# When the low parts of two weight chunks are made, in a three-block model kernel with a ring of weight slots

## The chip, the cores and the metric

The kernel runs on one core of one Trainium2 chip. The metric is the device time of one execution in microseconds, as the median of several runs; smaller is better. A profile of one execution stands beside it.

## The reference

A batch of one with 256 tokens (and 256 context tokens), width 1024. The first part is two layers, each with modulation, a mixer (attention), a layer norm, a gated feed-forward with a width-3 convolution, and a second layer norm. The second part puts 16 meta tokens ahead (272 tokens), and runs one layer of state-space mixing and a mixture of experts, with RMS norms. Everything is float32.

```python
def conv_ffn(h, w_gate, w_up, conv_w, conv_b, w_down):
    g = h @ w_gate
    ...
    return (jax.nn.silu(g) * (h @ w_up)) @ w_down

def first_block(...):
    for i in range(DEPTH):                       # 2 layers
        mods = modulation(c, w_mod[i], b_mod[i]) # one more set for the context
        h = x * (1.0 + sc1) + sh1
        o = even_mixer(...) if i % 2 == 0 else odd_mixer(...)
        x = layer_norm(ALPHA * x + gt1 * o, ln1_g[i], ln1_b[i])
        h = x * (1.0 + sc2) + sh2
        x = layer_norm(ALPHA * x + gt2 * conv_ffn(h, ...), ln2_g[i], ln2_b[i])
    return x

def second_block(x, meta_tokens, ...):
    h = concatenate([meta, x])
    u = rmsnorm(h, norm_mix)
    proj = u @ w_in
    h = h + concatenate([ssd_branch(proj...), short_conv_branch(proj...)]) @ w_out
    h = h + hier_moe(rmsnorm(h, norm_ffn), ...)
    return rmsnorm(h, norm_final)[:, N_META:]
```

## The kernel before

Activations lie feature-major: eight pieces of 128 features by 512, 256 or 272 tokens. The weights come as one list of chunks (`chunk_plan`), nearly all 128 x 2048 floats (1 MB), in the order of their use. SyncE walks the list and starts one DMA for each chunk into a ring of three slots, so chunk n takes the slot of chunk n - 3. It waits until `slot_free` says that this chunk is done with.

A float32 product is made from three products of rounded operands (type float32r): high by high, high part of the weight by low part of the input, low part of the weight by high part of the input (`mm3`). So each chunk is split: ScalarE copies it from the ring into WH (`act_high`, L461), VectorE subtracts to make WL (`dve_low`, L471); there are three places for split chunks. Once the low part is made, the chunk's ring slot is free. Chunks of the kinds `mod`, `qb` and `kvb` are not split (`whole`): TensorE reads them in the ring, and their slot is free when their product is done.

```python
        def slot_free(m):
            key = plan[m][0]
            if key[0] == "mod":
                return at("used", m)
            return at(*whole_free[key]) if whole[m] else at("low", m)
```

TensorE, ScalarE, VectorE and SyncE each run a program written out in order; they meet only at counted marks (`up`, `at`). The `ahead` argument of `act_high(e, n, ahead)` and `dve_low(e, n, ahead)` says how many chunks of the list, from n, are split at that point of the engine's program, unless they are already.

The places that matter, in order of time:
- Output projection and n00. `pe_out` multiplies `about` 0 to 3, VectorE adds each piece into X (`dve_out`, L800), and statistics of the layer norm follow. `pe_norm` spreads the mean and the deviation over the partitions (L602). Around them it multiplies modulation chunks of the second layer (`pe_mod`, L517): for n00 mod 1,0 and mod 1,1 ahead, mod 1,2 behind. VectorE and ScalarE make the eight normed pieces and split them (`dve_norm` L701, L719, L724; `act_norm` L669, L673).
- First feed-forward. The chunk list here reads about 3; gu 0,0; gu 0,1; mod 1,0; mod 1,1; mod 1,2; gu 0,2; mod 1,3; gu 0,3; and so on (gu l,f holds 128 columns of gate and of up of layer l). `four_tiles` multiplies gu 0,0 and gu 0,1 together, piece by piece as the norm delivers them; then each further chunk makes two tiles. The same list ends in 8 `down` chunks for each half.
- n01 and the second mixer's inputs: down 0,1,7; din 4; din 5; mod 1,21; mod 1,22; mod 1,23; din 6. `pe_norm` multiplies mod 1,21 and mod 1,22 ahead and mod 1,23 behind; `four_tiles` takes din 4 and din 5.
- n10 and the second feed-forward, dout 3; gu 1,0; gu 1,1; gu 1,2, with no modulation chunks between.
- n11 and block two: `pe_win` sums the squares of eight pieces (`pe_stat`, L597), spreads the root (L602), multiplies win 0 and win 1 in `four_tiles` and win 2 to 11 tile by tile; a small product by token (`pe_by_token`, L1726) lies between. The squares are VectorE's (L1824), the sum with the bias is ScalarE's (L2771).

Today, low parts are made ahead of a norm as follows. In `dve_out` of a norm's input, the last but one chunk makes low parts up to the second split chunk after it, and the last chunk does likewise. So the low parts of both chunks of `four_tiles` exist before the norm.

Of the kernel before, what the change touches and what calls it, by code (L numbers as in the profile page):

```python
# [17 lines left out]
NT = 272  # L18
# [324 lines left out]
def build(nc, wts, xin, meta, vecs, conds, csts, out):  # L343
# [5 lines left out]
    with ExitStack() as ctx:  # L349
# [129 lines left out]

        def mm3(e, o, w, cols, x, k, nk):  # L480
            e.matmul(o, w[0][:, cols], x[0], start=k == 0, stop=False)  # L481
            e.matmul(o, w[0][:, cols], x[1], start=False, stop=False)  # L482
            return e.matmul(o, w[1][:, cols], x[0], start=False, stop=k == nk - 1)  # L483
# [10 lines left out]
        def four_tiles(e, cs, o, x, names, arrive):  # L494
            ws = [weights(e, c) for c in cs]
            for k in range(8):
                e.wait_ge(*at(*arrive, k))
                for c, w, oc, name in zip(cs, ws, o, names):
                    for m in range(2):
                        t = mm3(e, oc[m], w, slice(256 * k + 128 * m, 256 * k + 128 * m + 128), at_k(x, k), k, 8)  # L500
                        if k == 7:
                            t.then_inc(*(up("used", c) if m else up("tile", *name)))
# [127 lines left out]
        def pe_norm(e, N, between=()):  # L630
            for c in between[:-1]:
                pe_mod(e, 1, c)
            b = bank(e, "mean", N.tag)
            e.wait_ge(*at("variance.mean", N.tag))
            pe_spread(e, b, N.MU, N.q).then_inc(*up("mean", N.tag))
            banks.give(b, "scaled.centered", N.tag, 7)
            b = bank(e, "unit_dev", N.tag)
            e.wait_ge(*at("variance.inverse", N.tag))
            pe_spread(e, b, N.RS, N.q).then_inc(*up("mean.unit_dev", N.tag))
            banks.give(b, "scaled", N.tag, 7)  # L640
            for c in between[-1:]:
                pe_mod(e, 1, c)
# [143 lines left out]
        def dve_out(e, key, n, mt_per, l, gt, tag, nxt):  # L786
            for i in range(8 // mt_per):
                c = index[key + (i,)]
                dve_low(e, c, next_pair(c) if tag in NORMS and i >= 8 // mt_per - 2 else 2)
# [29 lines left out]
        def pe_ffn(e, F_):  # L819
            l, n = F_.l, F_.n  # L820
            H = parts(8, n)
            for half in range(2):
                if half == 0:
                    bs = [(bank(e, "gate", l, f), bank(e, "up", l, f)) for f in range(2)]
                    four_tiles(e, [index["gu", l, f] for f in range(2)], [[ps[:, b, 0:n] for b in bf] for bf in bs], H,
                               [("gu", l, f) for f in range(2)], ("norm_low", F_.arrive))
# [17 lines left out]

        def act_ffn(e, F_, put_off):
            l, n = F_.l, F_.n
            H2 = ffn_parts(n)
            for half in range(2):
                for i in range(HALF):
# [3 lines left out]
                    act_high(e, c)  # L853
# [19 lines left out]
        def dve_ffn(e, F_, gt_from, fold_next=None):  # L873
# [3 lines left out]
            for half in range(2):  # L877
                for i in range(HALF):
# [5 lines left out]
                    dve_low(e, c)  # L884
# [806 lines left out]
        def pe_stat(e, tag, j, sq):  # L1691
            e.wait_ge(*at("stat_square" if tag == "mix" else "stat_square_act", tag, j))
# [17 lines left out]
        def dve_stat_norm(e, tag, gname, dst):  # L1710
# [6 lines left out]
            for j in range(8):  # L1717
                e.scalar_tensor_tensor(out=dst[:, j, :], in0=R[:, j, :], scalar=V(gname, j),
                                       in1=B("stat_spread", tag)[:, 0:NT], op0=ALU.mult,
                                       op1=ALU.mult).then_inc(*up("normed", tag, j))  # L1720

        def pe_by_token(e, tag, w, n, row, arrive):
# [5 lines left out]
            banks.give(b, "token.row", tag)  # L1728
            b = bank(e, "tokens.turned", tag)
# [25 lines left out]
        def pe_win(e):  # L1755
            bank(e, "stat", "mix")
            for j in range(8):
                pe_stat(e, "mix", j, ZS)
            bs = [[bank(e, "win", 2 * i + m) for m in range(2)] for i in range(2)]
            four_tiles(e, [index["win", i] for i in range(2)], [[ps[:, b, 0:NT] for b in bi] for bi in bs], YP,  # L1760
                       [("win", 0), ("win", 2)], ("u_low",))
            for i in range(12):
# [8 lines left out]
                if i == 1:  # L1771
                    pe_by_token(e, "dt", "wdt", 16, sc_root, "mix")

        def act_win(e):
            e.wait_ge(*META)
            e.wait_ge(*at("residual", "n11", 7))
            e.activation(R[:, :, 0:16], MT.rearrange("p (a b) -> p a b", a=8), ACT.Copy).then_inc(*up("joined"))
            act_stat_root(e, "mix")
# [3 lines left out]
            for i in range(12):  # L1782
# [4 lines left out]
                if i == 1:  # L1787
                    act_time(e)
# [29 lines left out]
        def dve_win(e):  # L1818
# [3 lines left out]
            for j in range(8):  # L1822
                e.wait_ge(*at("residual", "n11", j))
                e.tensor_tensor(ZS[:, j, 16:NT], R[:, j, 16:NT], R[:, j, 16:NT],  # L1824
                                ALU.mult).then_inc(*up("stat_square", "mix", j))
            dve_stat_norm(e, "mix", "nmix", UB)
            for j in range(8):
                e.wait_ge(*at("u_high", j))
                e.tensor_tensor(YP[1][:, j, :], UB[:, j, :], YP[0][:, j, :].bitcast(F32),
                                ALU.subtract).then_inc(*up("u_low", j))  # L1830
            for i in range(12):
# [4 lines left out]
                if i == 1:  # L1836
                    dve_time(e)
# [10 lines left out]
        def dve_time(e):  # L1848
            dve_token_row(e, "dt", 16, sc_root)
# [514 lines left out]
        def pe_gather(e):  # L2364
            pe_by_token(e, "ffn", "rw", 20, RSTD, "ffn")
            for c in range(3):
# [363 lines left out]
        def tensor_program(e):  # L2730
# [9 lines left out]
            pe_norm(e, N10)  # L2740
            pe_ffn(e, F1)
            pe_norm(e, N11)
# [11 lines left out]
        def scalar_program(e):  # L2754
# [14 lines left out]
            for j in range(8):  # L2769
                e.wait_ge(*at("scaled", "n11", j))  # L2770
                e.activation(R[:, j, 16:NT], N11.T8[:, j, :], ACT.Identity, bias=V("ln2b1", j),  # L2771
                             scale=1.0).then_inc(*up("residual", "n11", j))
# [139 lines left out]
```

## Time and profile before

| | us |
|---|---|
| median of 3 runs | 1879.32 (1878.71 to 1881.64) |
| the profiled execution | 1878.08 |
| its span in the profile | 1876.3 |
| TensorE busy | 1750.7 |
| VectorE busy | 1075.4 |
| ScalarE busy | 827.8 |
| mean granted TensorE clock | 0.951 of full |

Starts in the timelines are microseconds from the start of the span. A matmul's shown duration includes its passage through the array; products in a row overlap, so the distance between starts is what one costs. The granted clock of 1.00 is 2.4 GHz, 0.50 is 1.2 GHz; a value between means that the stretch saw both.

### The profile page before, as it was taken

The page shows a single profiled execution, that of the slowest core. Times are in us where ns is not written, and L with a number is a line of the kernel's source. Part 1 is how long each engine was busy: PE and PEld are TensorE (multiplying, and loading weights), DVE is VectorE, ACT ScalarE, POOL GpSimd, SP SyncE. Part 2 cuts the span into 40 slices and gives each one's busy share as a digit, 9 for nine tenths or more (in the row PEclk, how much of TensorE's full clock was granted, in tenths as well). Part 3 has the DMA queues.
Part 4 walks back from the last instruction along what each step waited for, and adds up shares of the span by engine and source line. Part 5 has one row for each costly group of instructions (what it writes and reads, how often), then busy time and mean ns, then how long its engine had stood idle before and what let it go on. Part 6 is the DMA issues. An engine that isn't in the chain of part 4 may idle for free.

```text
span 1876.3 us, 24577 instructions
## 1 busy us (share of the span) xinstructions
PE 1750.7 (93%) x10048; PEld 1375.2 (73%) x10048; DVE 1075.4 (57%) x1616; ACT 827.8 (44%) x1186; POOL 0.9 (0%) x5
## 2 busy tenths in 40 slices
PE   5988999979999999999988999789999989999997
PEld 2744446657787787699468999789876957877775
DVE  2255665434433444543965666647766645888886
ACT  3334443433312332523535544445444325767664
POOL 0000000000000000000000000000000000000000
PEclk7999999989999999999888999889998877999998
DMA  9311334234333433323022464433322306989993
GB/s 357 121 34 46 113 113 157 90 112 179 138 121 139 175 133 125 134 90 113 1 73 104 154 206 160 160 112 135 113 91 90 123 12 261 364 326 354 339 332 133
DMA packets 42676, 287.72 MB, mean 153 GB/s; under 512 B 4784, under 2 KB 5936, under 8 KB 11200
## 3 DMA queue, kind: packets, MB, share of 16 engines
q1 hardware_dynamic: 42384, 285.97, 42.0%
q8 instruction: 82, 1.34, 0.3%
q14 instruction: 34, 0.28, 0.0%
q10 hardware_dynamic: 144, 0.06, 0.0%
q0 software_dynamic: 32, 0.07, 0.0%
HBM read 285.03 MB, written 1.05 MB: 152 GB/s over the span
## 4 chain that ended last, share of the span: by engine, by line
PE 83%; DVE 8%; ACT 5%; issue 2%; DMA 1%; SPq 0%; DVEq 0%; ACTq 0%
PE ps L481 17%; PE ps L482 16%; PE ps L483 16%; PE ps L2486 5%; PE ps L2456 2%; PE ps L2457 2%; PE ps L2460 2%; PE ps L1399 2%; DVE WL L471 2%; PE ps L517 2%; PE ps L2392 2%; DMA ring<-wts 1%; PE ps L1368 1%; PE ps L1300 1%; PE ps L597 1%
## 5 line engine op out<-in xcount | busy, mean ns | idle before, releaser
L481 PE MATMUL ps<-HH,WH 128*128 128x512 f32 (+2 forms) x1552 | 522.4, 337 | 36.7 <-DVE WL L471 23.2
L471 DVE TENSOR_TENSOR WL<-ring,WH 128x2048 fp32r<-128x2048 f32 (+2 forms) x191 | 413.3, 2170 | 172.0 <-ACT WH L461 171.6
L483 PE MATMUL ps<-HH,WL 128*128 128x512 f32 (+2 forms) x1552 | 510.7, 329 | 0.0
L482 PE MATMUL ps<-HL,WH 128*128 128x512 f32 (+2 forms) x1552 | 510.5, 329 | 0.0
L461 ACT ACTIVATE WH<-ring 128x2048 fp32r<-128x2048 f32 (+2 forms) x191 | 346.6, 1817 | 224.9 <-DMA ring<-wts 83.5
L481 PEld LDWEIGHTS ps<-HH,WH 128*128 128x128 f32 x1552 | 301.5, 194 | 88.8 <-issue 36.2
L483 PEld LDWEIGHTS ps<-HH,WL 128*128 128x128 f32 x1552 | 301.4, 194 | 23.3
L482 PEld LDWEIGHTS ps<-HL,WH 128*128 128x128 f32 x1552 | 301.9, 195 | 22.4 <-issue 0.5
L481 PE MATMUL ps<-parts,WH 128*128 128x512 f32 (+1 forms) x352 | 119.7, 340 | 0.0
L482 PE MATMUL ps<-parts,WH 128*128 128x512 f32 (+1 forms) x352 | 118.4, 336 | 0.0
L483 PE MATMUL ps<-parts,WL 128*128 128x512 f32 (+1 forms) x352 | 118.3, 336 | 0.0
L2456 PE MATMUL ps<-WH,HH 128*128 128x512 f32 x256 | 103.6, 405 | 6.4 <-DVE WL L471 6.4
L2457 PE MATMUL ps<-WL,HH 128*128 128x512 f32 x256 | 101.2, 395 | 0.0
L2460 PE MATMUL ps<-WH,HL 128*128 128x512 f32 x256 | 101.0, 395 | 0.0
L800 DVE SCALAR_TENSOR_TENSOR X<-ps,modv,X 128x256 f32<-128x256 f32 x72 | 32.6, 481 | 118.0 <-PE ps L483 117.9
L471 DVE TENSOR_TENSOR WL<-arena,WH 128x2048 fp32r<-128x2048 f32 x38 | 86.3, 2286 | 3.8 <-ACT WH L461 3.7
L461 ACT ACTIVATE WH<-arena 128x2048 fp32r<-128x2048 f32 x38 | 72.8, 1919 | 31.4 <-PE ps L2460 16.5
L2486 PE MATMUL ps<-WH,parts 128*128 128x512 f32 x256 | 72.9, 396 | 2.7 <-DVE parts L2575 1.5
L481 PEld LDWEIGHTS ps<-parts,WH 128*128 128x128 f32 x352 | 66.8, 190 | 8.9 <-issue 1.8
L483 PEld LDWEIGHTS ps<-parts,WL 128*128 128x128 f32 x352 | 66.8, 190 | 7.0
L482 PEld LDWEIGHTS ps<-parts,WH 128*128 128x128 f32 x352 | 66.8, 190 | 6.7
L517 PE MATMUL ps<-ring,scond 128*32 128x512 f32 x384 | 56.5, 667 | 13.1 <-DMA ring<-wts 6.6
(332 smaller groups left out, 2191.8 us busy)
## 6 DMA issues: line engine op xcount, KB each, us to landing
ring<-wts SPq DMA_DIRECT2D x206, 1024.0 KB, 5.0
arena<-wts SPq DMA_DIRECT2D x38, 1024.0 KB, 7.0
ring<-wts SPq DMA_DIRECT2D x32, 704.0 KB, 4.0
X<-xin SPq DMA_DIRECT2D x4, 512.0 KB, 9.5
cst<-csts SPq DMA_DIRECT2D x1, 1373.0 KB, 15.4
ring<-wts SPq DMA_DIRECT2D x3, 384.0 KB, 3.1
out<-arena SPq DMA_DIRECT2D x2, 512.0 KB, 2.9
ring<-wts SPq DMA_DIRECT2D x1, 640.0 KB, 3.5
```

What stands on the lines that cost most here:

```text
L461: e.activation(split_parts(i)[0], raw(i), ACT.Copy).then_inc(*up("high", i))
L471: e.tensor_tensor(lo, raw(i), hi.bitcast(F32), ALU.subtract).then_inc(*up("low", i))
L481: e.matmul(o, w[0][:, cols], x[0], start=k == 0, stop=False)
L482: e.matmul(o, w[0][:, cols], x[1], start=False, stop=False)
L483: return e.matmul(o, w[1][:, cols], x[0], start=False, stop=k == nk - 1)
L517: t = e.matmul(ps[32 * j:32 * j + 32, b, :], scond[:, 2 * k:2 * k + 32], w[:, 512 * j:512 * j + 512], start=k == 0, stop=k == 7)
L1399: t = e.matmul(ps[r:r + 64, b, 0:256], v, PTA[:, j % 2, kt, :], start=kt == 0, stop=kt == n - 1)
L2392: t = e.matmul(ps[:, b, :], UT[p][0:n, c, 128 * k:128 * k + 128], SLOTP[0:n, c, :], start=c == 0, stop=c == 2)
L2456: e.matmul(ps[:, b, :], XG[0][:, k, g], w[0][:, s], start=k == 0, stop=False)
L2457: e.matmul(ps[:, b, :], XG[0][:, k, g], w[1][:, s], start=False, stop=False)
L2460: t = e.matmul(ps[:, b, :], XG[1][:, k, g], w[0][:, s], start=False, stop=k == 7)
L2486: t = e.matmul(ps[:, bs[n], :], HTE[p][:, z, hs], w[q][:, s], start=first and p == q == 0, stop=last and p == 1)
```

## The change

1. `dve_out` makes the low part of the chunk after next only at the last but one chunk of a norm's input; at the last chunk it makes no more than the next one's.
2. `four_tiles` waits at first only for the low part of its first chunk and the high part of its second. In each step it makes 6 products with the first and 4 with the high part of the second; the 16 products with the second's low part follow at the end.
3. In the feed-forwards both ScalarE and VectorE, before tiles 0 and 1, go on splitting up to the chunk two further (`through`); modulation chunks on the way don't count.
4. `pe_warm` makes products whose result nobody reads: 3 in the norms n10 and n11 ahead of the deviation's spread, 6 ahead of the second feed-forward's tiles, 2 ahead of each of the eight sums in block two and 6 ahead of its tiles.
5. The squares for block two move from VectorE to ScalarE and are taken from the scaled piece with the bias; the joining sums are spread around the root. The low parts of block two's inputs are interleaved with their scaling.
6. The turned token rows and the step sizes follow chunk 2 and not chunk 1.

```diff
+        def pe_warm(e, b, n, x):
+
+            for _ in range(n):
+                e.matmul(ps[:, b, :], x[:, 0:128], x[:, 0:512], start=True, stop=True)
+
...
         def four_tiles(e, cs, o, x, names, arrive):
-            ws = [weights(e, c) for c in cs]
+            w = weights(e, cs[0])
+            e.wait_ge(*at("high", cs[1]))
+            v = split_parts(cs[1])
             for k in range(8):
                 e.wait_ge(*at(*arrive, k))
-                for c, w, oc, name in zip(cs, ws, o, names):
-                    for m in range(2):
-                        t = mm3(e, oc[m], w, slice(256 * k + 128 * m, 256 * k + 128 * m + 128), at_k(x, k), k, 8)
-                        if k == 7:
-                            t.then_inc(*(up("used", c) if m else up("tile", *name)))
+                for m in range(2):
+                    t = mm3(e, o[0][m], w, slice(256 * k + 128 * m, 256 * k + 128 * m + 128), at_k(x, k), k, 8)
+                    if k == 7:
+                        t.then_inc(*(up("used", cs[0]) if m else up("tile", *names[0])))
+                for m in range(2):
+                    for h in range(2):
+                        e.matmul(o[1][m], v[0][:, 256 * k + 128 * m:256 * k + 128 * m + 128], at_k(x, k)[h],
+                                 start=k == h == 0, stop=False)
+            e.wait_ge(*at("low", cs[1]))
+            for m in range(2):
+                for k in range(8):
+                    t = e.matmul(o[1][m], v[1][:, 256 * k + 128 * m:256 * k + 128 * m + 128], at_k(x, k)[0], start=False,
+                                 stop=k == 7)
+                t.then_inc(*(up("used", cs[1]) if m else up("tile", *names[1])))
...
-        def pe_norm(e, N, between=()):
+        def pe_norm(e, N, between=(), warm=None):
...
+            if warm is not None:
+                weights(e, warm)
+                pe_warm(e, b, 3, split_parts(warm)[0])
             e.wait_ge(*at("variance.inverse", N.tag))
...
-                dve_low(e, c, next_pair(c) if tag in NORMS and i >= 8 // mt_per - 2 else 2)
+                dve_low(e, c, next_pair(c) if tag in NORMS and i == 8 // mt_per - 2 else 2)
...
+                    if l:
+                        pe_warm(e, bs[0][0], 6, split_parts(index["gu", l, 0])[0])
...
+        def through(l, f):
+            return index["gu", l, f + 2] + 1 - index["gu", l, f]
+
...
-                    act_high(e, c)
+                    act_high(e, c, through(l, f) if f < 2 else 3)
...
-                    dve_low(e, c)
+                    dve_low(e, c, through(l, f) if f < 2 else 2)
...
         def pe_stat(e, tag, j, sq):
-            e.wait_ge(*at("stat_square" if tag == "mix" else "stat_square_act", tag, j))
+            if tag == "mix" and j == 0:
+                e.wait_ge(*at("stat_square.meta"))
+            e.wait_ge(*at("stat_square_act", tag, j))
...
             for j in range(8):
+                if tag == "mix":
+                    e.wait_ge(*at("residual", "n11", j))
                 e.scalar_tensor_tensor(out=dst[:, j, :], in0=R[:, j, :], scalar=V(gname, j),
...
+                if then and j > 1:
+                    then(j - 2)
...
             for j in range(8):
+                pe_warm(e, bs[0][0], 2, w)
                 pe_stat(e, "mix", j, ZS)
-            bs = [[bank(e, "win", 2 * i + m) for m in range(2)] for i in range(2)]
+            pe_warm(e, bs[0][0], 6, w)
...
+                if i == 2:
+                    pe_token_turn(e, "dt", 16, sc_root)
...
         def act_win(e):
+            for j in range(8):
+                e.wait_ge(*at("scaled", "n11", j))
+                e.activation(ZS[:, j, 16:NT], N11.T8[:, j, :], ACT.Square, bias=V("ln2b1", j),
+                             scale=1.0).then_inc(*up("stat_square_act", "mix", j))
+            for j in range(2):
+                act_joined(e, j)
+            act_stat_root(e, "mix")
             e.wait_ge(*META)
-            e.wait_ge(*at("residual", "n11", 7))
             e.activation(R[:, :, 0:16], MT.rearrange("p (a b) -> p a b", a=8), ACT.Copy).then_inc(*up("joined"))
-            act_stat_root(e, "mix")
+            for j in range(2, 8):
+                act_joined(e, j)
...
-            pe_norm(e, N10)
+            pe_norm(e, N10, (), index["gu", 1, 0])
             pe_ffn(e, F1)
-            pe_norm(e, N11)
+            pe_norm(e, N11, (), index["win", 0])
```

## Rows read from the trace of the kernel before

**Rows 1.** The page, busy time of each engine: share of the span and instructions.
```profile
PE 1750.7 (93%) x10048; PEld 1375.2 (73%) x10048; DVE 1075.4 (57%) x1616; ACT 827.8 (44%) x1186; POOL 0.9 (0%) x5
```

**Rows 2.** Windows 400 to 755 us, their sum: length, then busy us of each engine.
```profile
sum 355.00, PE 355.00 PEld 275.88 DVE 143.76 ACT 108.29 POOL 0.00; mean PE 118.33 PEld 91.96 DVE 47.92 ACT 36.10 POOL 0.00
```

**Rows 3.** Timelines around n00: start, us, engine, line, instruction, idle time before and releaser.
```profile
333.71 2.29 DVE L471 TENSOR_TENSOR WL<-ring,WH 128x2048 fp32r<-128x2048 f32 x1 [4.02 <-ACT WH L461]
...
336.03 0.33 SPq L2832 DMA_DIRECT2D ring<-wts  x1
...
347.02 1.07 PE L517 MATMUL ps<-ring,scond 128*32 128x512 f32 x8
350.83 0.47 PE L481 MATMUL ps<-HH,WH 128*128 128x512 f32 x1 [2.75 <-DVE HL L724]
...
361.95 0.69 DVE L724 TENSOR_TENSOR HL<-arena,HH 128x512 fp32r<-128x512 f32 x1 [0.95 <-ACT HH L673]
...
374.06 0.39 PE L483 MATMUL ps<-HH,WL 128*128 128x512 f32 x1
...
382.44 3.69 ACT L461 ACTIVATE WH<-ring 128x2048 fp32r<-128x2048 f32 x2
...
386.71 0.79 PE L481 MATMUL ps<-HH,WH 128*128 128x512 f32 x1 [12.26 <-DVE WL L471]
...
400.68 1.06 PE L517 MATMUL ps<-ring,scond 128*32 128x512 f32 x8
```

**Rows 4.** The tile ring from 330 to 425 us: how long its transfers took.
```profile
DMA to landing us min/median/max: 4.8/6.5/8.9
```

**Rows 5.** Timelines around n01, columns as in rows 3.
```profile
762.29 1.06 PE L517 MATMUL ps<-ring,scond 128*32 128x512 f32 x8
...
777.23 0.69 DVE L724 TENSOR_TENSOR HL<-arena,HH 128x512 fp32r<-128x512 f32 x1 [0.96 <-ACT HH L673]
...
789.40 1.03 PE L531 MATMUL ps<-cond,mrow 128*128 128x8 f32 x8 [1.28 <-ACT mrow L544]
```

**Rows 6.** Windows: stretch and length, busy us of each engine, PEclk, DMA share, GB/s.
```profile
766.10:789.40 23.30, 22.01 (x97) 17.95 (x97) 12.62 (x18) 15.14 (x24) 0.00 (x0) 1.00 0.24 91
386.70:400.60 13.90, 13.89 (x48) 10.98 (x48) 3.65 (x3) 1.41 (x2) 0.00 (x0) 0.78 0.20 75
998.00:1012.20 14.20, 14.20 (x96) 14.10 (x96) 6.12 (x18) 8.73 (x16) 0.00 (x0) 0.79 0.00 1
1017.10:1024.70 7.60, 7.53 (x50) 7.53 (x51) 5.00 (x8) 4.17 (x7) 0.00 (x0) 0.78 0.58 186
1224.50:1238.80 14.30, 14.24 (x97) 14.13 (x97) 4.58 (x8) 2.40 (x3) 0.00 (x0) 0.84 0.21 74
...
1209.00:1214.70 5.70, 0.00 (x0) 0.00 (x0) 5.70 (x17) 3.95 (x8) 0.00 (x0) 0.50 0.00 0
```

**Rows 7.** Timelines of the second feed-forward's start.
```profile
1004.24 0.43 DVE L724 TENSOR_TENSOR HL<-arena,HH 128x256 fp32r<-128x256 f32 x1 [0.52 <-ACT HH L673]
...
1017.17 0.39 PE L481 MATMUL ps<-HH,WH 128*128 128x256 f32 x1 [4.87 <-DVE WL L471]
...
1026.04 2.29 DVE L471 TENSOR_TENSOR WL<-ring,WH 128x2048 fp32r<-128x2048 f32 x1
...
1030.55 0.42 DVE L893 TENSOR_TENSOR arena<-arena,ps 128x256 f32<-128x256 f32 x1 [1.11 <-PE ps L483]
...
1031.80 2.28 DVE L471 TENSOR_TENSOR WL<-ring,WH 128x2048 fp32r<-128x2048 f32 x1
```

**Rows 8.** Timelines from the last sum into X to block two's sums.
```profile
1201.71 2.29 DVE L471 TENSOR_TENSOR WL<-ring,WH 128x2048 fp32r<-128x2048 f32 x1 [3.80 <-ACT WH L461]
1203.92 0.48 DVE L800 SCALAR_TENSOR_TENSOR X<-ps,modv,X 128x256 f32<-128x256 f32 x1
...
1204.46 0.32 PE L597 MATMUL ps<-X,cst 128*32 128x64 f32 x8 [2.68 <-DVE X L800]
...
1214.79 2.72 PE L597 MATMUL ps<-arena,cst 128*32 128x68 f32 x64 [5.93 <-DVE arena L1824]
```

## What was predicted

> **What bounds the kernel now.** I read the page first: TensorE is busy for 93% of the span [rows 1], so a microsecond counts only where TensorE idles, where its clock is low, or where it is newly made to wait. Next the list of TensorE's waits by stretch, which names four places that the diff touches: the two norms of block one's first layer (n00, n01), the first tiles of the second feed-forward (after n10), and the step from n11 into block two. The windows show the opposite in between: from 400 to 755 us TensorE is busy for all 355 of 355 us [rows 2]. A delay ahead of such a stretch isn't absorbed; it arrives whole at the end. Last, the timelines of the four places, with the DMA queue beside the engines, because the diff moves a VectorE instruction that frees a slot of the weight ring.
>
> **Part 1: the second chunk's low part is no longer made ahead of the norm.** In `dve_out` the condition goes from "the last two chunks" to "the last but one". So the low part of the chunk after next (gu 0,1 before n00; din 5 before n01; gu 1,1; win 1) is made only behind `dve_norm`. `four_tiles` is rewritten to need it late, which serves TensorE. But `slot_free` gives a ring slot back on that same low part, slots go round by three, and three places behind gu 0,1 stands mod 1,2, three behind din 5 stands mod 1,23. `pe_norm` multiplies exactly that chunk last, ahead of `four_tiles`. The trace shows the link: the low part runs 333.71 to 336.00 and the DMA is issued at 336.03 [rows 3]. Today that is early, and mod 1,2 is multiplied at 347.02 without a wait.
>
> *At n00.* VectorE's last piece of the norm starts at 361.95 and takes 0.69 [rows 3], so it ends at 362.6. Nothing in that norm waits for the held product, so it runs as before. Low part 2.29: 364.9. Issue to landing: shortest here 4.8, median 6.5 for overlapping transfers [rows 4]; this one is at the head of its queue, I take 5.0: 369.9. The product with mod 1,2 takes 1.1 (row of its twin, [rows 5]): 371.0. Four tiles are 96 products; at full clock such a group held TensorE 22.0 us, 0.227 each [rows 6]: 21.8. TensorE has then idled over 20 us. After today's 12.26 us of idling the next 13.9 us ran at a granted 0.78 [rows 3, 6], a loss of 13.9 x 0.22 = 3.1. Four tiles end at 395.9, against 374.4 today. What is won back: the 12.26 us wait for gu 0,2's low part goes, since `through` splits that chunk before tile 0. (It lands behind mod 1,2, its parts take 1.9 (half of the pair's 3.69) and 2.3, and tiles last till 396: hidden with some 15 us to spare.) Its 48 products take 10.9: 406.8, where the row of today has the next product at 400.68. So **+6.1**, and TensorE is full until 755 [rows 2].
>
> *At n01.* Last piece ends 777.23 + 0.69 = 777.9; low part 780.2; landing 785.2; product 786.3; four tiles 21.8 and 3.1 for the clock: 811.2. Today the small products behind the tiles start at 789.40 [rows 5], and here nothing is won back: those tiles run at a granted 1.00 [rows 6] and the wait behind them is 1.28, which is inside the difference. **+21.8.** Queued behind the held product on TensorE is all of the second mixer; VectorE and ScalarE wait for its tiles.
>
> The two sum to +27.9. Bounds: landing 4.8 gives 27.5; landing 8.9 twice [rows 4] gives 35.7; a clock that doesn't fall gives 21.7.
>
> **Part 2: the second feed-forward.** No modulation chunk lies here, so part 1 hurts nothing: the slot of gu 1,1 goes to gu 1,4, wanted 20 us later. Four tiles run at a granted 0.79 for 14.2 us [rows 6], 11.2 at full clock. The norm's last piece ends at 1004.7; two low parts more end at 1009.3, about when the tiles do, so the wait of 4.87 [rows 7] goes. The most to win is that, 1.7 of slow clock behind it (7.6 x 0.22, [rows 6]) and the 3.0 in the tiles: 9.6. But VectorE is next. A round of its gate work and one low part takes 5.76 with 1.11 of waiting for TensorE in it [rows 7], so at least some 5.0 with latencies. The low part of gu 1,4 comes behind three rounds: 1009.3 + 3 x 5.1 + 2.3 = 1026.9. Today it starts at 1026.04 and ends at 1028.3, and TensorE begins gu 1,4 two chunks of 5.76 and 1.7 of slow clock behind 1017.17, at 1030.4. So at most 3.5 of the 9.6 survive, less what the clock costs in the new short wait. The nine fillers of 0.227 lie in idle time, except some 0.2 ahead of the spread. **-3**, bounds -6 and 0.
>
> **Part 3: into block two.** (a) win 1's low part (1201.71, 2.29) stands today in front of the last sum into X at 1203.92, and TensorE waits 2.7 for that [rows 8]; gone, 2.4 is won. With a shorter wait the spreads of the mean run faster too, some 0.8. (b) Squares move to ScalarE beside the scaling, so the eight sums need not follow at VectorE's pace: they took 2.72 [rows 8]. But `stat_square.meta` still comes from VectorE behind all eight scalings, TensorE's first sum waits for it, and fourteen filler products stand between the eight sums: 14 x 0.227 = 3.2 at full clock, up to 6.4 at half, besides 1 to 2 of sums. The granted clock is 0.50 there today [rows 6]. I reckon 6.6, some 3.5 more than now, which eats the gain of (a). The Trainium skill ("TensorE: Matmul & The Clock Gate", Part 1: The HAM clock gate) has it that the slow clock is the default and that activity lifts it; by that rule the fillers would soon run at full clock, (b) would cost some 2 less and this part would come to about -6. The row of 0.50 is from a stretch without products, so it doesn't contradict. (c) Interleaved low parts start the four tiles after three scaled pieces and not after eight: about 2.5 won; the tiles themselves are 14.3 at 0.84, so up to 2.3 of slow clock, I take 1. (d) The turned token rows go behind chunk 2: 0.6 won, perhaps 0.8 lost later because ScalarE and VectorE then wait for them with win 4's split queued behind. Sum: -2.4 - 0.8 + 3.5 - 2.5 - 1 - 0.6 + 0.3 = -3.5; with (b) uncertain both ways, **-4**, bounds -8 and +1.
>
> **The sum.** 27.9 - 3 - 4 = +20.9. The profiled execution took 1878.08 (span 1876.3 and 1.8 around it), so 1899.0; the median of the runs is 1.2 above it, so 1900.
>
> **The rivals.**
> *The transfers land abreast.* mod 1,2 is followed at once by two transfers that have been held behind it; at n01 two likewise. If they share the rings, the first lands near the longest row, 8.9 instead of 5.0, twice: +7.8, 1908. For: the median is already 6.5 when transfers overlap. Against: today's first of three lands soon enough not to be waited for. The Trainium skill ("DMA: Bandwidth & Descriptors", Queues, rings and completion order) says that descriptors of one ring start in order, but that a later one may finish its write before an earlier one; by that rule this case is open, and no row here settles it.
> *The fillers don't pay.* Clock stays low through the fillers and the sums queue behind them: parts 2 and 3 yield nothing, 1907. For: 0.50 granted through that stage today. Against: the fillers themselves are activity.
> *The fillers pay fully.* Parts 2 and 3 near their bounds, -12 instead of -7: 1895; decides if the clock stays up from the mean's spread on.
> *The other side: the held chunk isn't waited for.* If mod 1,2 and mod 1,23 were in the ring by the time of their product, n00 would win the 12.26 and 3.1 of clock, n01 the 1.28, and with -7 the kernel would come to about 1856. It decides at a landing before 347 and 762, that is if the slot were freed by anything but the low part. Against it stand the issue 0.03 us behind the low part's end [rows 3] and the code of `slot_free`; for it nothing that I found.
> *No effect.* Gains and the held chunks cancel: it would need only one of the two waits and all bounds of parts 2 and 3.
>
> **Chances.** My forecast 0.72; abreast 0.09; fillers don't pay 0.07; pay fully 0.05; other side 0.05; no effect 0.02. A difference under 0.2% (3.8 us) is about what a measurement of this kernel can't tell from none. So slower 0.93, same 0.02, faster 0.05. The range 1890 to 1909 takes in the two costlier cases, the cheaper one and the bounds of the landing and of parts 2 and 3; only the last two cases are left out.
>
> **What would show it.** In the profile after: at n00 TensorE idle from about 348 to 370, released by the DMA into the ring ahead of the product at L517; the low part of gu 0,1 at 362 and not at 333; no 12 us wait behind the four tiles; at n01 an idle of some 22 us in front of that same line. Granted clock near 0.5 at the start of both groups of tiles. In FFN two the wait of 4.87 gone and a shorter one two or three chunks later. In block two the last sum into X right behind its product, and the eight sums stretched by fillers. The prediction is wrong if the product L517 of these two chunks isn't preceded by idling, or if TensorE's waits between the four places grow, which I cost at nothing.

## The result and the profile after

| | before | changed |
|---|---|---|
| median | 1879.38 us (1878.71 to 1881.64, 4 runs) | 1911.58 us (1906.90 to 1912.74, 4 runs) |
| span of the profiled execution | 1876.3 | 1910.2 |
| TensorE busy | 1750.7 | 1763.6 |
| mean granted clock | 0.951 | 0.947 |

The changed kernel is slower: ratio 1.0165, interval 1.0152 to 1.0179. That is 32 us, where 21 were forecast; the median is 2.6 us above the range.

The page, busy time of each engine, for the changed kernel:
```profile
PE 1763.6 (92%) x10082; PEld 1378.3 (72%) x10082; DVE 1072.1 (56%) x1608; ACT 831.2 (44%) x1194; POOL 0.9 (0%) x5
```
Against [rows 1], TensorE is busy 12.9 us longer with only 34 instructions more, while the span grew by 33.9. So about a third of the loss is products that take longer or are fillers, and two thirds is idling of TensorE.

The changed kernel's timelines around n00:
```profile
364.88 2.28 DVE L471 TENSOR_TENSOR WL<-ring,WH 128x2048 fp32r<-128x2048 f32 x1
367.20 1.28 SPq L2879 DMA_DIRECT2D ring<-wts  x3
372.16 1.93 PE L533 MATMUL ps<-ring,scond 128*32 128x512 f32 x8 [22.73 <-DMA ring<-wts]
374.61 1.91 ACT L461 ACTIVATE WH<-ring 128x2048 fp32r<-128x2048 f32 x1 [10.37 <-DMA ring<-wts]
394.22 3.79 PE L516 MATMUL ps<-HH,WL 128*128 128x512 f32 x16
408.81 1.06 PE L533 MATMUL ps<-ring,scond 128*32 128x512 f32 x8
```
The low part that stood at 333.71 in [rows 3] now begins at 364.88. The DMA is issued 0.04 us behind its end, and the product with mod 1,2 starts when that lands, after 22.73 us without work. The product itself takes 1.93 and not 1.06. The last row answers to the last of [rows 3]: 408.81 against 400.68.

The changed kernel's timelines around n01:
```profile
785.96 2.28 DVE L471 TENSOR_TENSOR WL<-ring,WH 128x2048 fp32r<-128x2048 f32 x1
793.13 1.94 PE L533 MATMUL ps<-ring,scond 128*32 128x512 f32 x8 [22.64 <-DMA ring<-wts]
818.26 0.95 PE L547 MATMUL ps<-cond,mrow 128*128 128x8 f32 x8
```
The same picture. The small products behind the tiles start at 818.26, against 789.40 in [rows 5].

The changed kernel's chain that ended last, from 340 to 440 us (start, us, engine and line):
```profile
364.97 2.21 DVE WL L471
367.20 4.92 DMA ring<-wts
372.16 1.93 PE ps L533 x8
```
This is the forecast chain: low part, transfer, product. The chain names the link that the list of waits ("DMA ring<-wts") leaves out: the transfer was late because VectorE was.

Its start of the second feed-forward:
```profile
1049.66 0.39 PE L486 MATMUL ps<-HH,WH 128*128 128x256 f32 x1 [0.51 <-DVE WL L471]
1057.38 2.28 DVE L471 TENSOR_TENSOR WL<-ring,WH 128x2048 fp32r<-128x2048 f32 x1
1059.72 0.39 PE L486 MATMUL ps<-HH,WH 128*128 128x256 f32 x1 [4.04 <-DVE WL L471]
```
The wait of 4.87 in [rows 7] is gone, and one of 4.04 stands two chunks later, in front of gu 1,4.

Its way into block two:
```profile
1232.48 0.48 DVE L819 SCALAR_TENSOR_TENSOR X<-ps,modv,X 128x256 f32<-128x256 f32 x1 [3.54 <-PE ps L488]
...
1241.94 0.46 PE L613 MATMUL ps<-arena,cst 128*32 128x68 f32 x8 [4.98 <-DVE arena L1872]
1242.32 1.22 PE L483 MATMUL ps<-WH 128*128 128x512 f32 x2
1243.48 0.46 PE L613 MATMUL ps<-arena,cst 128*32 128x68 f32 x8
...
1252.70 0.46 PE L613 MATMUL ps<-arena,cst 128*32 128x68 f32 x8
1254.29 1.95 PE L618 MATMUL ps<-X,cst 128*128 128x68 f32 x8 [1.14 <-DVE X L1739]
1255.99 2.90 PE L483 MATMUL ps<-WH 128*128 128x512 f32 x6
```
[Rows 8] with the 31.0 us of delay that this kernel has by then would put the last sum into X at 1234.9; it stands at 1232.48. But one sum of eight small products and two fillers take 1.54 us (1241.94 to 1243.48), so the eight end at 1253.1: 11.2 us, against 2.72 in [rows 8].

Windows of the changed kernel (length, busy us of each engine, PEclk, DMA share, GB/s):
```profile
372.00:386.00 14.00, 13.84 (x52) 9.95 (x53) 2.29 (x1) 1.91 (x1) 0.00 (x0) 0.78 0.73 281
1031.60:1043.50 11.90, 11.85 (x99) 11.88 (x100) 10.99 (x21) 9.72 (x16) 0.00 (x0) 1.00 0.17 50
...
1236.00:1242.00 6.00, 1.02 (x10) 0.58 (x13) 5.41 (x15) 3.72 (x8) 0.00 (x0) 0.97 0.00 0
1242.00:1244.50 2.50, 2.50 (x20) 1.35 (x20) 0.00 (x0) 1.03 (x3) 0.00 (x0) 0.50 0.02 7
1244.50:1254.00 9.50, 8.65 (x60) 3.73 (x58) 0.43 (x1) 0.78 (x3) 0.00 (x0) 0.50 0.00 0
1254.00:1258.00 4.00, 3.71 (x13) 3.35 (x14) 1.81 (x6) 3.26 (x9) 0.00 (x0) 0.50 0.00 0
1258.00:1262.00 4.00, 4.00 (x29) 3.81 (x28) 4.00 (x11) 2.35 (x7) 0.00 (x0) 0.90 0.00 0
```
Behind the wait at n00 the first 14 us of tiles run at 0.78, the loss that was reckoned. In the second feed-forward three fillers in the norm and six ahead of the tiles go with a clock of 1.00, and 96 products take 11.9 us instead of 14.2 at 0.79 [rows 6]. In block two the clock is down at the end of TensorE's wait for VectorE (4.98 us), and it stays at 0.50 for 16 us of nearly unbroken products.

**Where the 33.9 us of span lie.** The delay of the changed kernel is read at landmarks: the same product's start in both profiles, subtracted. A part of the kernel costs what the delay grows by across it. Landmarks by their start in the kernel before; the last is in block two's last stage.

| profile | 303 | 401 | 789 | 850 | 970 | 1174 | 1311 | 1867 |
|---|---|---|---|---|---|---|---|---|
| changed | 2.3 | 8.1 | 28.9 | 28.8 | 33.6 | 31.0 | 31.6 | 33.9 |
| changed, again | 2.5 | 8.2 | 28.8 | 28.7 | 32.1 | 30.6 | 29.4 | 29.1 |
| before, again | 3.0 | 2.9 | 3.0 | 3.0 | 3.0 | 2.9 | 2.9 | 3.0 |

So, in us: n00 (303 to 401) +5.8, n01 +20.8, second mixer (850 to 970) +4.8, second feed-forward -2.6, block two's start (1174 to 1311) +0.6, the rest of block two +2.3. The first 2.3 are no effect of the change: the kernel before has them too when profiled again.

### The profile page after: what moved, and what is told of

It is laid out like the page before. It is cut to its first block, busy times and chain, and to the rows that moved or that the text cites. A ratio compares the mean times of both kernels' runs of the same rounds, so it can differ in the third digit from the quotient of the medians.

```text
span 1910.2 us, 24644 instructions
## 1 busy us (share of the span) xinstructions
PE 1763.6 (92%) x10082; PEld 1378.3 (72%) x10082; DVE 1072.1 (56%) x1608; ACT 831.2 (44%) x1194; POOL 0.9 (0%) x5
## 4 chain that ended last, share of the span: by engine, by line
PE 81%; DVE 10%; ACT 5%; issue 2%; DMA 2%; DVEq 0%; ACTq 0%; SPq 0%
PE ps L486 16%; PE ps L487 15%; PE ps L488 15%; PE ps L2537 5%; DVE WL L471 2%; PE ps L2507 2%; PE ps L1423 2%; PE ps L2511 2%; PE ps L2508 2%; PE ps L533 2%; DMA ring<-wts 2%; PE ps L2443 2%; PE ps L1392 1%; PE ps L1324 1%; PE ps L613 1%
## 5 line engine op out<-in xcount | busy, mean ns | idle before, releaser
L486 PE MATMUL ps<-HH,WH 128*128 128x512 f32 (+2 forms) x1488 | 498.7, 335 | 13.3 <-DVE WL L471 10.2
L488 PE MATMUL ps<-HH,WL 128*128 128x512 f32 (+2 forms) x1488 | 487.0, 327 | 0.0
L487 PE MATMUL ps<-HL,WH 128*128 128x512 f32 (+2 forms) x1488 | 486.6, 327 | 0.0
L486 PEld LDWEIGHTS ps<-HH,WH 128*128 128x128 f32 x1488 | 287.1, 193 | 66.8 <-issue 28.3
L488 PEld LDWEIGHTS ps<-HH,WL 128*128 128x128 f32 x1488 | 287.1, 193 | 22.0
L487 PEld LDWEIGHTS ps<-HL,WH 128*128 128x128 f32 x1488 | 287.5, 193 | 21.0 <-issue 0.5
L461 ACT ACTIVATE WH<-arena 128x2048 fp32r<-128x2048 f32 x38 | 72.8, 1919 | 31.6 <-PE ps L2511 16.2
```

What stands on the lines that cost most here:

```text
L461: e.activation(split_parts(i)[0], raw(i), ACT.Copy).then_inc(*up("high", i))
```

## The experiments

**Two profiles more**, of the kernel before and of the changed one, unaltered.

> The kernel before, unchanged, for a second profile. All four kernels so far, also the one whose program is the old one up to n00, are 1.6 us late against the first profile of before between 288 and 303 us, and 2 to 5 us late through the second mixer, where no code changed. If that is chance of the first profile, the second one of before shows 1.6 us at 303 and 2 or more us over the mixer as well; if the change does it, the second profile lies on the first.

> The changed kernel once more, for a second profile. In the first one the second mixer (850 to 971 us of the kernel before), where no code changed, took 4.8 us more; in two profiles of the kernel before it took the same to 0.1 us, in the other changed kernels 1.5 to 5 more. If that is chance of the clock, this profile may show anything from 0 to 5; if it belongs to the kernel, 4 to 5 again.

Measured 1881.11 and 1907.44, one execution each. The profile of before shifts by 3.0 us ahead of 303 us and then agrees with the first to 0.1 us at every landmark. Window 288 to 303 us, first profile of before and then its second:
```profile
288.00:303.00 15.00, 13.15 (x69) 10.02 (x70) 6.95 (x15) 4.59 (x4) 0.00 (x0) 1.00 0.59 211
```
```profile
288.00:303.00 15.00, 12.70 (x56) 9.46 (x57) 7.07 (x16) 4.88 (x5) 0.00 (x0) 0.89 0.62 230
```
The granted clock there was 1.00 once and 0.89 once. The second profile of the changed kernel repeats n00 and n01 (5.7 and 20.6), but has 3.4 in the mixer and -1.2 into block two. In its stretch of sums and fillers the clock rose earlier:
```profile
1241.50:1251.00 9.50, 9.50 (x68) 4.43 (x68) 0.00 (x0) 1.08 (x3) 0.00 (x0) 0.50 0.01 2
1251.00:1257.00 6.00, 4.40 (x36) 3.12 (x29) 2.88 (x7) 4.21 (x12) 0.00 (x0) 0.93 0.00 0
```
So a difference of under some 2 us in one such part isn't to be explained from one profile of each kernel.

**Low parts early again, all else as changed.**
```diff
-                dve_low(e, c, next_pair(c) if tag in NORMS and i == 8 // mt_per - 2 else 2)
+                dve_low(e, c, next_pair(c) if tag in NORMS and i >= 8 // mt_per - 2 else 2)
```


> The changed kernel with one line put back: the last chunk ahead of a norm again makes the low part of the chunk after next, so mod 1,2 and mod 1,23 can be in the ring in time. If the held ring slot is the cause, TensorE's two waits of 22.7 and 22.6 us at the modulation products go and the wait of 12.3 us behind the first four tiles stays gone: n00 comes to some 15 us less than before the change where it now stands at 5.8 more, n01 to 1 less where it stands at 20.7 more, the step into block two loses 2.4 again; together 1911.6 - 21 - 22 + 2.4 = 1871 us (1865 to 1876). If the held slot is not the cause (late tiles, the new product order or the fillers are), the time stays above 1900.

Measured 1873.12 (1871.91 to 1876.16), ratio 0.9968 (0.9955 to 0.9980). Timeline and TensorE's waits around n00:
```profile
349.47 1.06 PE L533 MATMUL ps<-ring,scond 128*32 128x512 f32 x8
```
```profile
PE ps L486 <- DVE HL L743: 2.8, 1, 2.8
```
The product isn't waited for, n00 gains 15.4 us instead of costing 5.8, n01 costs 0.2. The one character undoes 38.5 us, which is more than the whole loss. But its price is seen too: into block two this kernel loses 6.2 us.

**Only the later low parts, all else as before.** The same line of the kernel before, `>=` made `==`.

> The kernel before with only that one line changed, all else old. Held-slot theory: n00 +21.5 us (the wait for mod 1,2, and the 12.3 us wait behind the tiles stays), n01 +21.8, the second feed-forward +9 (the old four tiles need gu 1,1's low part, now made at 1004.7 to 1007.0, and start there and not at 998.0), block two +2: 1879.4 + 54 = 1934 us (1925 to 1940). Rival, that late low parts only move work within idle time: below 1890.

Measured 1935.40 (1932.57 to 1938.58), ratio 1.0291 (1.0274 to 1.0308). TensorE's waits from 340 to 440 us:
```profile
PE ps L517 <- DMA ring<-wts: 22.6, 1, 22.6
PE ps L481 <- DVE WL L471: 12.3, 1, 12.3
```
n00 costs 20.6 and n01 21.6. So at n00 the rest of the change (gu 0,2 split ahead of the tiles) gives back 14.8 of its own; at n01 it gives back under 1, since nothing was lost there before. In the second feed-forward, where no modulation chunk lies, the late low part costs 9.5 by itself: its 4.87 of [rows 7] has become 11.32.

**Low parts early at n01 only, late at n00, n10 and n11.**
```diff
-... if tag in NORMS and i == 8 // mt_per - 2 else 2)
+... if tag in NORMS and (i == 8 // mt_per - 2 or i > 8 // mt_per - 2 and tag == "n01") else 2)
```


> The changed kernel with the low part made early at n01 alone. Held-slot theory: n01's term goes (20.7 + 1.3), n00's stays (5.8 more than before the change): 1911.6 - 22 = 1889.6 us (1886 to 1893). If the two waits fed one another, the time would leave that range.

Measured 1891.65 (1891.14 to 1893.71), ratio 1.0066 (1.0049 to 1.0082). n01 costs 0.0 and n00 5.6: the two waits are independent, each with its own slot.

**Low parts early at n00 and n01, late at n10 and n11.** The same line with `tag in ("n00", "n01")`.

> The changed kernel with the low parts made early at n00 and n01 only; at n10 and n11, where no modulation chunk waits for the slot, they stay late. Theory: against the kernel with all of them early, 2.4 us less ahead of n11's mean, and the fillers between the sums find TensorE less cold there (the step into block two cost that kernel 6.2 us and the changed one 0.5): 1873.1 - 5 = 1868 us. Rival, that the late part costs at n10 or n11 too: 1873 or more.

Measured 1867.62 (1865.64 to 1869.48), ratio 0.9937 (0.9921 to 0.9954). Against the kernel with all of them early, 5.5 us less, and the landmarks put it where (a) of part 3 had it: into block two 0.6 instead of 6.2. Of these 5.6 us, 2.4 are there by the last sum into X, as (a) reckoned, and 4.7 by block two's first sum. At n10 the same move shows no gain: the second feed-forward yields 1.9 us here and 2.5 with the low part early. So the later low part is a gain into block two; that no `whole` chunk lies three places behind makes it harmless at n10 in the changed kernel, and in the old one it cost 9.5 there.

**The held product behind the tiles.** All low parts late, but the products with mod 1,2 and mod 1,23 stand behind `four_tiles`.
```diff
@@ pe_norm
-            for c in between[-1:]:
-                pe_mod(e, 1, c)
@@ pe_ffn, behind four_tiles
+                    if l == 0:
+                        pe_mod(e, 1, MODS_FIRST[-1])
@@ behind n01's four_tiles
+            pe_mod(e, 1, MODS_LAST[-1])
```


> The changed kernel with the low parts as late as the change has them, but the products with mod 1,2 and mod 1,23 moved behind the four tiles, so that TensorE doesn't need the held chunks there. If late low parts harm only through the slot, the loss goes without touching them: four tiles start when the norm delivers, near 353 and 754 us, and the kernel comes to 1911.6 - 43 = 1868 us, up to 3 more because the last modulation row now follows the tiles. If making low parts late costs by itself (ScalarE and VectorE are busy when gu 0,2 lands), above 1880.

Measured 1874.62 (1872.18 to 1880.15, 10 runs), ratio 0.9976 (0.9965 to 0.9986). The theory of the slot holds: the transfer is as late as before, and 37 us come back, more than the 32 that were lost, because nobody waits for it. The number was missed by 4 to 7. With the product gone from its place, TensorE waits 3.7 instead of 2.8 us for the first piece (its waits from 340 to 420 us below), and n00 gains 12.9 instead of 15.4. A wait of 1.1 for a low part follows right behind 401. n01 costs 3.2, and another 1.6 right behind it, where the granted clock is 0.71 from 784.2 to 790.0. The wait for the first piece:
```profile
PE ps L486 <- DVE HL L741: 3.7, 1, 3.7
```

**Without the fillers between the sums.** The line `pe_warm(e, bs[0][0], 2, w)` in `pe_win` goes.

> The changed kernel without the sixteen filler products between block two's eight sums (nothing of the result depends on them). In the profile of the change the sums stretch over 11.2 us at a granted clock of 0.50, each pair of fillers holding TensorE 1.15 us. Theory: they are pure cost there: the eight sums then take 3.1 at half clock (1.5 at full), so 8 us less, 1903.5 us. Rival, that they buy back their cost by bringing the clock up for the tiles behind: the tiles run at 0.9 granted now; without fillers up to 3 us slower, net 5 us less, 1906.5 us.

Measured 1899.05 (1895.86 to 1901.54), ratio 1.0101 (1.0084 to 1.0118): 12.5 us less than the changed kernel. Timeline of its sums:
```profile
1240.24 2.04 PE L613 MATMUL ps<-arena,cst 128*32 128x68 f32 x64 [5.70 <-DVE arena L1871]
1243.42 1.95 PE L618 MATMUL ps<-X,cst 128*128 128x68 f32 x8 [1.13 <-DVE X L1739]
```
The sums take 2.04 us instead of 11.2, and the spread behind them 1.95 as with fillers. In the changed kernel's first profile sixteen fillers bought no clock at all; in its second the clock was up by the eighth sum and for the spread, which took 1.08. Between the landmarks at 1174 and 1311 the delay falls by 7.9 (+0.6 to -7.3); 1.1 were already there at 303, 1.5 come in the mixer and 2.9 behind 1311; the second feed-forward gives 1.1 less. So some 8 us are the price of the fillers by the trace, and the other 5 lie in parts that also differ between two profiles of one kernel.

**Without any filler.** `pe_warm` goes from the norm, the second feed-forward and `pe_win`.

> The changed kernel without any filler product. Theory: the fillers of the two norms and those ahead of the second feed-forward's tiles hold the clock up there (granted 1.00 where it was 0.79 for 14.2 us and the spreads at 0.53), worth 2 to 4 us, so this is 2 to 4 us slower than the kernel without the sum fillers alone, about 1906. Rival, that VectorE's chain bounds the second feed-forward's start whatever the clock: equal to that kernel within 1 us.

Measured 1900.72 (1900.49 to 1901.66), ratio 1.0111 (1.0094 to 1.0128): 1.7 more than with the fillers ahead of the tiles alone, intervals overlapping. The window of its four tiles in the second feed-forward:
```profile
1031.00:1045.00 14.00, 12.50 (x85) 12.53 (x86) 12.05 (x25) 10.41 (x19) 0.00 (x0) 0.76 0.19 61
```
The clock there is 0.76 instead of 1.00, yet that part yields 1.5 us, against 2.6 with fillers and 1.5 in the changed kernel's other profile. That fits the forecast that faster tiles run into VectorE's gate work; whether these fillers are worth anything, these runs don't tell.

**The best of it: early at n00 and n01, late at n10 and n11, no fillers between the sums.**

> The same without the sixteen fillers between the sums. Held slot and sum fillers are separate terms, so they add: 1868 - 12 = 1856 to 1860 us, the best so far. If the fillers are needed once the other waits are gone, above 1864.

Measured 1858.50 (1858.16 to 1860.27), ratio 0.9889 (0.9873 to 0.9906). That is 9.1 less than with the fillers between the sums, the second time that taking them out gives about this much; into block two the landmarks show -7.4 where they showed +0.6, so 8.0 by the trace, as 7.9 above.

**The same, with twenty fillers in one piece ahead of the first sum.**
```diff
+            pe_warm(e, bs[0][0], 20, w)
             for j in range(8):
-                pe_warm(e, bs[0][0], 2, w)
                 pe_stat(e, "mix", j, ZS)
```


> The same, with twenty fillers in one piece ahead of the first sum, that is in the 5 us in which TensorE idles behind the deviation's spread, and none between the sums. Theory: the clock is still up there (0.97 granted from 1236 to 1242 in the changed kernel) and falls because of the idling, not for want of fillers between the sums; then the eight sums and the spread of the root run at full clock, 1.5 + 0.9 us less, and the four tiles lose no 2 us: 2 to 4 us less than without. Rival, that the sums' gaps lower the clock again at once: equal within 1 us, or worse by the fillers that overrun.

Measured 1856.29 (1856.20 to 1858.46), ratio 0.9879 (0.9863 to 0.9896). Timeline and windows:
```profile
1190.66 4.82 PE L483 MATMUL ps<-WH 128*128 128x512 f32 x20
1196.35 1.15 PE L613 MATMUL ps<-arena,cst 128*32 128x68 f32 x64 [0.87 <-DVE arena L1872]
1198.65 1.44 PE L618 MATMUL ps<-X,cst 128*128 128x68 f32 x8 [1.14 <-DVE X L1739]
```
```profile
1190.60:1196.30 5.70, 4.88 (x23) 3.71 (x21) 5.41 (x15) 3.62 (x8) 0.00 (x0) 1.00 0.01 3
1196.30:1200.20 3.90, 2.70 (x73) 2.57 (x74) 0.59 (x2) 3.77 (x11) 0.00 (x0) 0.87 0.00 0
```
The fillers lie in the idle time before the sums (4.82 us, then a wait of 0.87), the clock is still up when the sums come, and those take 1.15 instead of 2.04, the spread 1.44 instead of 1.94. That is 1.4 us by these two rows, 2.6 between the landmarks at 1174 and 1311 (-10.0 against -7.4) and 2.2 by the medians, whose intervals overlap: the rows show the gain, the medians alone don't. It is the fastest kernel of this study, 23 us below the one before.

**Only a delay.** The kernel before, with thirty filler products ahead of n01's four tiles and nothing else changed.
```diff
+            wd = weights(e, index["din", 4])
+            for _ in range(30):
+                e.matmul(ps[:, b[0][0], :], wd[0][:, 0:128], wd[0][:, 0:512], start=True, stop=True)
```


> The kernel before with thirty filler products ahead of the four tiles of din 4 and din 5, and nothing else: 6.8 us of TensorE, of which 2.7 lie in its wait, so everything behind n01 comes 4.1 us later. Theory of chance, that what the mixer pays depends on where the clock's ups and downs fall: the mixer takes 0 to 5 us more, not foreseeable. Theory that a plain delay costs only itself: 1880 + 4.1 = 1884 us and 0 over the mixer.

Measured 1886.97 (1886.57 to 1890.63), ratio 1.0043 (1.0028 to 1.0057). The fillers cost 4.0 at their place, as foreseen. Right behind n01 another 1.6 follows, which nobody foresaw: the granted clock is 0.84 from 794.0 to 804.6, where the kernel before has 1.00 from 789.4 to 800.0. (The kernel with only the later low parts and the one with the product behind the tiles lose 1.5 and 1.6 there; the changed one doesn't.) Then the second mixer, of which no line differs, costs 3.4. Ahead of the edit, across n00, this profile gives back 1.8 without any cause in the program, which is once more what one profile differs from the next. Windows of 20 us in that mixer at the same products, the kernel before and then the changed one:
```profile
894.00:904.00 10.00, 8.46 (x19) 4.60 (x20) 8.57 (x19) 5.57 (x16) 0.00 (x0) 0.53 0.00 0
904.00:914.00 10.00, 10.00 (x33) 5.24 (x31) 9.22 (x20) 6.85 (x19) 0.00 (x0) 0.79 0.00 0
```
```profile
922.80:932.80 10.00, 7.26 (x20) 3.46 (x20) 8.57 (x19) 5.58 (x17) 0.00 (x0) 0.83 0.00 0
932.80:942.80 10.00, 9.18 (x26) 5.56 (x28) 7.41 (x17) 6.95 (x19) 0.00 (x0) 0.66 0.00 0
```
The delayed kernel has the changed one's course (0.83 and 0.66 in the two windows), the one with the product behind the tiles that of before (0.54 and 0.78). Timelines from the first of these products on, the kernel before and then the changed one:
```profile
895.53 5.94 PE L1591 MATMUL ps<-arena,X 64*128 64x512 f32 x10 [2.64 <-ACT arena L1614]
```
```profile
924.32 4.99 PE L1615 MATMUL ps<-arena,X 64*128 64x512 f32 x10 [2.64 <-ACT arena L1638]
...
930.31 0.63 PE L1664 MATMUL ps<-cst,arena 128*128 128x128 f32 x4 [0.41 <-DVE arena L1656]
...
933.62 3.41 PE L1615 MATMUL ps<-arena,X 64*128 64x512 f32 x6 [1.64 <-ACT arena L1638]
```
In the course of before the low clock lies on these scores, TensorE is busy through the second window, and the mixer takes its 120.5 us; both profiles of before and the kernel with the product behind the tiles have it. In the other one the ten products start at the same place (924.32 less the delay of 28.8), behind the same wait of 2.64, but the clock is soon up and they take 4.99 instead of 5.94. TensorE comes too early to what follows, waits 0.41 and 1.64, and the clock is low again later. So the clock differs first, and the additional wait for ScalarE's exponentials comes after it. The waits of TensorE in the mixer, the kernel before and then the changed one:
```profile
PE ps L1591 <- ACT arena L1614: 3.5, 3, 2.6
```
```profile
PE ps L1615 <- ACT arena L1638: 5.9, 4, 2.6
```
The changed kernel in both its profiles, the delayed one, the one late at n00 and the two with fewer fillers have this 5.9 and cost 3.3 to 4.8. The kernels with early low parts at n00 and n01 wait 5.5 to 5.8 and cost 1.5 to 5.0, the one with only the later low parts waits 4.3 and costs 3.4; so the wait alone doesn't give the cost.

## Why the prediction was partly right

**What bounds, and part 1: right.** The held slot is the loss. n00 +5.8 against +6.1, n01 +20.8 against +21.8. The steps hold too: low part 364.88 (foreseen 362.6), the DMA issued at once, 4.92 to landing (5.0), the clock behind it 0.78 (0.78). The product took 1.93 and not 1.1, since it runs at the low clock as well, and the issue came 2.3 later; the tiles were quicker in turn: 408.81 less the 2.3 of before 303 is 406.5, where 406.8 was reckoned. Undoing just this (the low parts early again) gives back 38.5 us, and doing just this costs 55.

**The rival "abreast": wrong for the first of three.** Three transfers are issued together at 367.20 with a median of 7.0 us to landing (below), but the first was there in 4.92, and the product waits for that one alone. At n01 it is the same: the low part ends at 788.24, and the product starts at 793.13.
```profile
ring<-wts SPq DMA_DIRECT2D x3, 1024.0 KB, 7.0
```
The Trainium skill ("DMA: Bandwidth & Descriptors", Queues, rings and completion order) says that a later descriptor may finish its write before an earlier one, and so left open whether the transfer in front lands first. Here it did, after 4.92 us at n00 and 4.82 at n01.

**Part 2: right.** -2.6 against -3 (again -1.5). The new wait stands at gu 1,4, whose products start 4.3 us earlier than in the kernel before, once the delay of 33.6 is taken off (1059.72 - 33.6 = 1026.1, against 1030.4), and part of that is given back in the chunks behind it. VectorE's chain was sized well: that chunk's low part ends at 1059.66, which is again 1026.1, where 1026.9 was reckoned.

**Part 3: the term that failed is (b).** "I reckon 6.6" for the eight sums with fillers; they took 11.2. The count was right (14 fillers, and two ahead of the first). The size was not: each pair costs 1.15 us, 0.58 a filler, where the prediction had 0.227 at full clock and 0.46 at half. Seven pairs are 8.1 and eight sums of 0.38 another 3.1. Even the upper ends of its own terms, 6.4 for the fillers and 2 for the sums, make only 8.4. Half the clock doesn't explain all of it: six fillers in a row take 0.45 each at the same 0.50, so some 0.13 of each comes from standing between sums; why, no run shows. The clock stayed at 0.50 from 1242 to 1258 in one profile and to 1251 in the other, though TensorE was busy for 9.50 of 9.50 us. So the part came to +0.6 and -1.2, not -4. The prediction had this as its rival "the fillers don't pay" (0.07): for part 3 the rival is what happened, for part 2 it isn't. The prediction also took 2 us less for (b) as what the rule of the Trainium skill ("TensorE: Matmul & The Clock Gate", Part 1: The HAM clock gate) would give, that activity lifts the clock. The clock was lifted in the end (0.90 from 1258 to 1262), but by then the sums were done. (a) was right: the last sum into X comes 2.4 us earlier against the row of before, and the kernels with win 1's low part early and late differ by 5.6 into block two.

**The second step that failed: the second mixer was costed at nothing.** It took +4.8 and +3.4. The prediction said it would be wrong if TensorE's waits between the four places grew, and they did. The run that only delays shows that no part of the change has to act there: with fillers ahead of n01's tiles and 5.6 us of delay in all, the mixer runs into its other course. The timelines show the clock to differ first and the wait to follow. What decides where the clock falls, and so which delays lead to which course (+3.0 ahead of 303 us doesn't, the 5.6 does), stays open. The other 2.3 before 303 us and 2.3 at the end are no more than one profile of a kernel differs from its next.

Without either of the two terms, the 4.6 of (b) or the 4.8 of the mixer, the median would lie near 1907, inside the range. The main term, n00 and n01, was forecast at 27.9 and measured at 26.6.

The sum of the first profile: 20.9 forecast; +4.6 for block two's start, +4.8 mixer, +2.3 and +2.3 at the ends, -1.3 on part 1, +0.4 on part 2 make 34.0, against 33.9 of span.

## What to carry to other kernels

Before moving the instruction that gives back a buffer, list whose transfer takes that buffer next and where its consumer stands in program order: a 2.3 us subtraction moved behind a norm cost 22.7 us of waiting, twice, far from its own product. Give fillers to idle time ahead of the critical piece (20 there took 1.4 us off the rows behind them); sixteen between small sums cost 8. Compare two traces by the delay at common landmarks, and profile each kernel twice before explaining 2 to 5 us in a stage that no edit touches.

## What the runs showed of the hardware

- With 128x68 sums and 128x512 fillers in turn, the granted clock was 0.50 over 9.5 us of products (1241.5 to 1251.0, one profile) and over 16 us (1242 to 1258, another), behind 5 us of idling. A filler cost 0.58 us there in pairs between sums and 0.45 in a row of six; at 1.00, in a row of twenty, 0.24.
- Of three 1 MB transfers issued together, the first landed after 4.9 us while the median was 7.0.
- A stage of unchanged code took between 120.5 and 125.5 us over fourteen profiles; the kernel in which it only starts later (5.6 us) took 3.4 more. Of two profiles at the same products, the one whose clock was up sooner (ten products in 4.99 instead of 5.94 us) took longer in all, because waits followed.
